# Changing the planned order of TensorE in a two-layer hybrid trunk: margins, the first tile, and where mixer outputs are reloaded

## What is computed

```python
for layer in range(2):
    xn = rmsnorm(h, mix_norm_g[layer])
    if layer == 0:
        a, xb, gate_b, gate_c = split(xn @ ab_w_in)
        mix = concat(pool_mixer(a), gate_b * short_conv(gate_c * xb)) @ ab_w_out
    else:
        u, v, q, k, w = split(xn @ cd_w_in)          # u, v through gelu
        mix = concat(u * (W_s @ layernorm(v) + b), stick_breaking_attention(q, k, w)) @ cd_w_out
    h = h + mix
    h = h + square(relu(rmsnorm(h, mlp_norm_g[layer]) @ w1)) @ w2
return rmsnorm(h, final_norm_g)
```

## Time and profile before

| | us |
|---|---|
| median of three runs | 3223.5 (3199.45 to 3227.07) |
| the profiled execution | 3217.09 |
| its span on the slowest core | 3215.6 |
| spans of the eight cores | 3180.2 to 3215.6 |
| TensorE busy in the span | 2901.0 |
| VectorE, ScalarE, POOL busy | 1450.8, 1369.0, 1136.3 |

### The profile page before, as it was taken

The page is one execution under the profiler, slowest core; times in us unless marked ns, Lnnn a source line. Parts: engine busy times, 40 slices in busy tenths (PEclk is TensorE's granted clock), DMA queues, the critical chain, the costliest instruction groups (busy, mean ns, idle before and its releaser), DMA issues.

```text
span 3215.6 us, 46006 instructions; the slowest of 8 cores (3180.2 to 3215.6 us)
## 1 busy us (share of the span) xinstructions
PE 2901.0 (90%) x14778; PEld 1258.2 (39%) x15073; DVE 1450.8 (45%) x1829; ACT 1369.0 (43%) x2273; POOL 1136.3 (35%) x1622
## 2 busy tenths in 40 slices
PE   5999788899998889889898989998999989998997
PEld 2444333344343334333343433443444433443443
DVE  4410247432445444785545363435455565554102
ACT  2435233535335445347362336242463546263442
POOL 4211016233223344654442453332254444451110
PEclk9999899999999999999999999999999999999999
DMA  7799973444657999955655243455455585555222
GB/s 161 158 173 181 171 182 71 95 102 95 164 138 125 168 184 173 187 132 129 132 120 155 83 119 85 99 111 160 110 109 109 109 198 107 110 116 177 72 76 82
DMA packets 452826, 420.46 MB, mean 131 GB/s; under 512 B 310128, under 2 KB 326768, under 8 KB 452592
## 3 DMA queue, kind: packets, MB, share of 16 engines
q1 hardware_dynamic: 383328, 228.48, 32.0%
q0 software_dynamic: 69264, 189.02, 28.1%
HBM read 304.36 MB, written 89.13 MB: 122 GB/s over the span
## 4 chain that ended last, share of the span: by engine, by line
PE 56%; DMA 18%; DVE 10%; POOL 5%; issue 5%; ACT 3%; SPq 1%; DVEq 0%; POOLq 0%; ACTq 0%
PE ps L550 52%; DMA Wk<-Wq 12%; DVE P L1197 4%; POOL Wq L1211 3%; DMA oT<-stg 2%; DMA stg<-xT 2%; PE ps L1236 2%; DMA ring<-wblk 2%; ACT ps L540 2%; PE ps L1181 1%; DVE X_45 L660 1%; POOL ps_74 L903 1%; DVE stg L671 1%; SPq L543 1%; DVE st_58 L1012 1%
## 5 line engine op out<-in xcount | busy, mean ns | idle before, releaser
L550 PE MATMUL ps<-X_45,ring 128*128 128x512 bf16 x4742 | 1101.6, 383 | 26.2 <-DVE X_45 L660 8.5
L540 ACT ACTIVATE ps<-ps 128x512 f32<-128x512 f32 (+3 forms) x832 | 576.1, 697 | 595.1 <-PE ps L550 357.4
L1211 POOL TENSOR_TENSOR Wq<-P 128x1022 bf16<-128x1022 f32 (+2 forms) x320 | 528.0, 1650 | 534.4 <-DVE P L1197 527.3
L550 PEld LDWEIGHTS ps<-X_45,ring 128*128 128x128 bf16 x4864 | 460.6, 98 | 574.9 <-issue 62.8
L1197 DVE TENSOR_TENSOR_SCAN P<-ps,carry,zeros 128x512 f32<-128x512 f32 x384 | 489.8, 1279 | 375.3 <-ACT ps L540 357.6
L550 PE MATMUL ps<-mix,ring 128*128 128x512 bf16 x2481 | 600.8, 384 | 11.0 <-issue 4.0
L581 POOL DMA_DIRECT2D ring<-wbf x540 | 297.0, 552 | 815.8 <-PE ps L550 627.4
L691 DVE TENSOR_TENSOR h<-ps,h 128x512 f32<-128x512 f32 x384 | 263.1, 686 | 703.7 <-PE ps L550 702.3
L550 PE MATMUL ps<-ffB,ring 128*128 128x512 bf16 x2009 | 482.1, 380 | 2.2 <-issue 0.2
L1197 DVE TENSOR_TENSOR_SCAN P<-ps,zeros 128x128 f32<-128x128 f32 (+3 forms) x256 | 209.0, 820 | 416.3 <-ACT ps L540 403.1
L550 PE MATMUL ps<-X_44,ring 128*128 128x512 bf16 x1498 | 358.5, 389 | 15.0 <-DVE mix L874 4.9
(11 more groups left out here) (104 smaller groups left out, 1364.9 us busy)
## 6 DMA issues: line engine op xcount, KB each, us to landing
ring<-wbf POOLq DMA_DIRECT2D x540, 256.0 KB, 4.0
ring<-wblk POOLq DMA_DIRECT2D x180, 256.0 KB, 7.4
wbf<-ring SPq DMA_DIRECT2D x180, 256.0 KB, 5.7
stg<-xT SPq DMA_DIRECT2D x96, 256.0 KB, 5.8
h<-xT SPq DMA_DIRECT2D x64, 256.0 KB, 7.7
hsp<-h SPq DMA_DIRECT2D x64, 256.0 KB, 4.6
h<-hsp SPq DMA_DIRECT2D x64, 256.0 KB, 5.1
oT<-stg SPq DMA_DIRECT2D x64, 256.0 KB, 5.3
```

The costliest lines, as they stand in the source:

```text
L540: return Req("act", lambda e: e.activation(out=out, in_=in_, func=func, **kw), reads, writes, dur, bias=bias)
L550: ins = pe.matmul(out, lhsT=l, rhs=r, start=(first and i == 0), stop=(last and i == n - 1), skip_group_check=True)
L1211: yield Req("pool", lambda e: e.tensor_tensor(out=W3[:, :, 0:w - 1], in0=P[:, :, 1:w], in1=P[:, :, 0:w - 1], op=ALU.subtract), [LP], [LWq] ...
```

## The change

It changes what the planner assumes and what some fibers ask for:

- SEM is 0.18 instead of 0.10. A new field slack adds to it for single operations: 4.0 for the AV matmul, 0.5 for the scores, 1.0 for pooling, 0.6 for the gate matmul, 3.0 for the matmul that makes the gate's bias. The transposes are planned with 5.0 us instead of 4.0.
- Norms, pooling and gate matmuls ask with a tuple, which puts them at the head of the queue for a bank; pooling and gate matmuls also get a bias of -1.0.
- prefetch_x holds its norm until the planner's TensorE is 8 us past the last square.
- At the start, x comes ahead of the gate's constants (sgst), which lie where V will be; 48 matmuls on constants come first on TensorE, and one Ln on ScalarE; the first group of the first tile takes x tile by tile; the main fiber starts when the first half of x is asked for.
- An S stage that follows an M stage reads its mixer outputs from mix, loaded while that M stage computes V, K and Q. So free_x looks for the next F stage already there, and the norm of x for the second sequence moves from the stage S(0,0) into the one of F(0,1).

```diff
-SEM = 0.10
+SEM = 0.18
@@ ready
+        far = SEM + r.slack
-                f = d.fin + (0.0 if d.eng == eng and not d.dma else SEM)
+                f = d.fin + (0.0 if d.eng == eng and not d.dma else far)
@@ Machine.advance
+            elif isinstance(y, tuple):
+                f.state = "acq"
+                y = y[0]
+                y.queue.insert(0, f)
@@ alloc
+        self.sgst, _ = sb("sgst", [128, 1536], F32, self.off)
         self.V = sb("V", [128, 16, 512], BF16)
-        self.sgst, o = sb("sgst", [128, 1536], F32, o0)
@@ norm
-        bk = yield self.banks
+        bk = yield (self.banks,)
@@ prefetch_x
-                yield self.act(X[:, c, ts], self.stg[:, b, :], AF.Square, [self.Lstg[b]], [LX[c][t]], TT, False)
+                o = yield self.act(X[:, c, ts], self.stg[:, b, :], AF.Square, [self.Lstg[b]], [LX[c][t]], TT, False)
                 self.p_stg.free(b)
+            yield lambda: self.S.free["pe"] > o.fin + 8.0
@@ start_x
+        for c in range(8):
+            yield self.load_h(self.xT, None, 0, 0, 0, c)
+        self.xloading = True
+        for c in range(8):
+            yield self.load_h(self.xT, None, 0, 0, 1, c)
...
+            if t == 1:
+                yield lambda: self.main_t >= 16
@@ free_x
-        if self.hnext is not None:
-            kind, s, u = self.hnext
-            self.M.spawn(self.prefetch_x(s, u) if kind == "F" else self.load_mix(s, u), 0.6)
+        for (k0, _, _), (kind, s, u) in zip(self.stages[n:], self.stages[n + 1:]):
+            if kind == "F":
+                self.M.spawn(self.prefetch_x(s, u), 0.6)
+                return
+            if kind == "S" and k0 == "S":
+                self.M.spawn(self.load_mix(s, u, self.X[0], self.LX[0]), 0.6)
+                return
@@ chain_pool
-            b2 = yield self.banks
-            yield self.mm(self.bank(b2), [(self.cb[:, 384 + g * 128:512 + g * 128], PB[:])], [self.Lcb, L1], [self.Lbank[b2]])
+            b2 = yield (self.banks,)
+            yield self.mm(self.bank(b2), [(self.cb[:, 384 + g * 128:512 + g * 128], PB[:])], [self.Lcb, L1], [self.Lbank[b2]],
+                          bias=-1.0, slack=1.0)
@@ stage_F
+                    fine = (s, u, i, b, t) == (0, 0, 0, 0, 0)
@@ chain_v
-            b2 = yield self.banks
+            b2 = yield (self.banks,)
...
-            yield Req("pe", fn, [Lvn, self.Lwmt], [self.Lbank[b2]], 0.25)
+            yield Req("pe", fn, [Lvn, self.Lwmt], [self.Lbank[b2]], 0.25, bias=-1.0, slack=0.6)
@@ stage_M
+        if self.stages[sn + 1][0] == "S":
+            self.M.spawn(self.load_mix(*self.stages[sn + 1][1:], self.mix, self.Lmix, lambda: self.cdone == 2), -0.2)
         yield from self.need_attention(2 * s + u)
@@ att_item
-                  bias=-1.0)
+                  bias=-1.0, slack=0.5)
...
-                  key=("wk", k), lat=4.0, kb=w * 0.69)
+                  key=("wk", k), lat=5.0, kb=w * 0.69)
...
-        yield Req("pe", fn, [LWk] + [self.LV[c * 4 + j] for j in range(nb)], [self.Lbank[self.AVB]], nb * 0.115, bias=-1.0)
+        yield Req("pe", fn, [LWk] + [self.LV[c * 4 + j] for j in range(nb)], [self.Lbank[self.AVB]], nb * 0.115, bias=-1.0,
+                  slack=4.0)
@@ stage_S
-        yield from self.out_proj("S", s, u)
-        self.free_x()
+        src = (self.mix, self.Lmix) if self.stages[n - 1][0] == "M" else (self.X[0], self.LX[0])
+        yield from self.out_proj("S", s, u, *src)
+        if src[0] is self.X[0]:
+            self.free_x(n)
@@ setup
-        self.use_scratch("init")
+        bk = yield self.banks
+        yield Req("act", lambda e: e.activation(out=self.rtmp[:, 0, 0:1], in_=self.cf[:, 72:73], func=AF.Ln), [self.Lcf],
+                  [self.Lrt[0]], 1.5)
+        yield self.mm(self.bank(bk), [(self.cb[:, 0:128], self.cb[:, 384:896])] * 48, [self.Lcb], [self.Lbank[bk]])
+        self.banks.free(bk)
+        yield lambda: self.xloading
         yield self.dma(self.sgst[:], self.sg_d, [], [self.Lsgst], "sg", kb=768.0)
```

More of the change, by code:

```diff
@@ L543, in dma, with mm @@
         return Req("sp", lambda e: e.dma_start(out=out, in_=in_), reads, writes, 0.06, key=key, lat=2.0, kb=kb)
-    def mm(self, out, pairs, reads, writes, first=True, last=True, bias=0.0):
+    def mm(self, out, pairs, reads, writes, first=True, last=True, bias=0.0, slack=0.0):
         def fn(pe):
@@ L552, in fn @@
             return ins
-        return Req("pe", fn, reads, writes, len(pairs) * 0.2157, bias=bias)
+        return Req("pe", fn, reads, writes, len(pairs) * 0.2157, bias=bias, slack=slack)
     def block_order(self):
@@ L682, in norm_h @@
         yield lambda: ev[0] == 8
-        yield from self.norm(self.X[1], self.LX[1], t, None, gcol, dst)
+        yield from self.norm(self.X[1], self.LX[1], t, gcol, dst)
         done.add(t)
@@ L721, in dst @@
                 self.p_stg.free(b)
-            yield from self.norm(X, LX, t, None, 0, dst)
+            yield from self.norm(X, LX, t, 0, dst)
             self.xready.add((s, u, t))
@@ L727, in start_x @@
         X, LX = self.X[0], self.LX[0]
-        for t in range(2):
-            ts = slice(t * TT, (t + 1) * TT)
-            for c in range(8):
-                yield self.load_h(self.xT, None, 0, 0, t, c)
+        for c in range(8):
[3 more added lines that the diff above has]
+            yield self.load_h(self.xT, None, 0, 0, 1, c)
         for t in range(2):
@@ L736, in start_x @@
                 yield self.act(X[:, c, ts], self.h[:, c, ts], AF.Square, [self.Lh[c][t]], [LX[c][t]], TT, False)
-            yield from self.norm(X, LX, t, None, 0, self.to_X(t, 0))
+            if t == 1:
+                yield lambda: self.main_t >= 16
+            yield from self.norm(X, LX, t, 0, self.to_X(t, 0))
             self.xready.add((0, 0, t))
@@ L945, in stage_F @@
                 evs = (self.chain_pool(g, t, pp, seq0, tn),) + self.chain_conv(i, t, {"cv": cv}, seq0, tn)
+                L = [LX[k][t] for k in range(8)]
                 for b in range(4):
-                    yield from self.group(self.wpairs(sl[b], X, ts), [self.Lring[sl[b]]] + [LX[k][t] for k in range(8)],
-                                          evs[b])
+                    fine = (s, u, i, b, t) == (0, 0, 0, 0, 0)
+                    yield from self.group(self.wpairs(sl[b], X, ts), [self.Lring[sl[b]]] + ([] if fine else L), evs[b],
+                                          fine=L if fine else None)
                     if t == 1:
                         self.release(sl[b])
-        self.free_x()
-        yield from self.out_proj("F", s, u)
+        self.free_x(n)
+        yield from self.out_proj("F", s, u, self.mix, self.Lmix)
         nd = set()
@@ L988, in out_proj @@
             ts = slice(t * TT, (t + 1) * TT)
-            if kind == "F":
-                src, Lsrc = self.mix, self.Lmix
-                yield lambda: self.mixn[t] == 8 and self.hcount.get((kind, s, u, t)) == 8
-            else:
-                src, Lsrc = self.X[0], self.LX[0]
-                yield lambda: (s, u, t) in self.mready and self.hcount.get((kind, s, u, t)) == 8
+            yield lambda: (self.mixn[t] == 8 if kind == "F" else (s, u, t) in self.mready) and \
+                self.hcount.get((kind, s, u, t)) == 8
             for c in range(8):
@@ L1303, in setup @@
         bk = yield self.banks
-        yield self.mm(self.bank(bk), [(self.cb[:, 0:128], self.wmt[:])], [self.Lcb, self.Lwmt], [self.Lbank[bk]])
+        yield self.mm(self.bank(bk), [(self.cb[:, 0:128], self.wmt[:])], [self.Lcb, self.Lwmt], [self.Lbank[bk]],
+                      slack=3.0)
         for g in range(4):
@@ L1321, in main @@
             if kind == "F":
-                yield from self.stage_F(s, u)
+                yield from self.stage_F(n, s, u)
             elif kind == "M":
-                yield from self.stage_M(s, u)
+                yield from self.stage_M(n, s, u)
             else:
-                yield from self.stage_S(s, u)
+                yield from self.stage_S(n, s, u)
     def build(self):
```

31 lines of the change are left out of this document (17 added, 14 removed).

## The result

The changed kernel takes 3095.4 us (median of four runs, 3089.0 to 3098.3) where the kernel before, run beside it, takes 3217.0: a ratio of 0.9625, 95% interval 0.9575 to 0.9674, 122 us saved. Predicted were 3085 us in 3035 to 3165.

What follows compares the result with a forecast made beforehand. TensorE and its 314.6 us of waits bound the kernel. From 3217.1 us, -96 - 14 - 30 - 5 + 10 - 4 + 3 = -136 gives 3081, put at 3085 us for the median; range 3035 to 3165.

Steps and rivals of the forecast that it cites:

- AV, -96: Attention's last matmul waits 123.0 us for transposed weights Wk; going later in the order gains 96 us (60 to 115).
- the clock, -30: TensorE's granted clock: 110 us less idling at 0.28 us each gains 30 us (0 to 42).
- It is no fixed price: TensorE's lower clock loses 87 us over 314.6 idle us, 0.28 each; two stages show 0.38 and 0.
- Moved loads, +3 (0 to 20): Loads of x leave S(0,0) for a quieter stage, where they stand ahead of transposes: 3 us lost (0 to 20).
- the wait moves on: TensorE meets the next late producer (normed tiles, squares, conv, pooling); half of 96 us returns: 3142 us, chance 0.22.
- Gates, +10: Gate matmuls take a bank early; 21 of 32 stand one group earlier; 8 halves lose 10 us (0 to 38).
- banks run short: 104 small matmuls hold PSUM banks before their data is there, costing 240 us: 3311 us, chance 0.06.
- The sign of being wrong: On TensorE: the forecast is wrong if waits for evacuations of PSUM banks appear; no size given.
- Next norm, -14: Next unit's norm matmul, held until 8 us past the last square, no longer waits: 14 us gained (5 to 15.6).
- start, -5: Kernel start: x ahead of sgst, first group tile by tile, against warm-up and late sgst: 5 us gained (-10 to +7).
- The row that the prediction set against the rule: At 878 to 885 us a group fed tile by tile is followed by a clock of 0.53.
- Pooling, -4: Pooling matmuls, where waits for pb_76 and pb_73 cost 15.8 us: 4 us gained (0 to 15).

Runs made afterwards that it cites:

- AV's margin alone: Kernel before, with only slack 4.0 for the AV matmul and transposes planned with 5.0 instead of 4.0 us: ratio 0.9741, 3128 us.
- both parts: Kernel before, with AV's slack 4.0, transposes planned at 5.0 us, mixer outputs reloaded in the M stage and the earlier norm of x: ratio 0.9614, 3087 us.
- the old start: Changed kernel with the start of the kernel before: sgst ahead of x, no warm-up matmuls, no early Ln, first group not tile by tile: ratio 0.9635.
- All but the reload: Changed kernel with the moved loads put back: mixer outputs loaded inside the S stages, second sequence's norm of x in S(0,0): ratio 0.9811, 3157 us.
- all but AV's margin: Changed kernel with the AV matmul's slack back at 0 and transposes planned with 4.0 us: ratio 0.9872, 3173 us.
- SEM back: Changed kernel with SEM at 0.10 instead of 0.18, all slacks kept: ratio 0.9688, 3117 us.

## Why the prediction was right, and where it was right by luck

The time was right; the sum behind it had two terms wrong by about 40 us each, in opposite directions. That they cancelled was luck.

**AV, -96, and most of the clock, -30.** Waits for Wk fell by 113 us in the change and by 100 alone (in the mean of the cores by 102 and 92), within the bounds (60 to 115). But 96 us of idling and its 0.28 of clock, 123 us together, is too much for this part: alone it gave 83. The step that failed is the price of the clock. Idle time per core fell by 75 us with AV's margin alone, from 260 to 185 in the mean of the cores by the rows of waits, and the mean granted clock not at all. 19.4 us of quicker work came in the end, but with the reload. The table shows a part of the reason: with AV's margin alone F(1,0) keeps a long wait, and the lower clock takes 17 us there; with both parts it takes 7. That is 10 of the 28 us by which the two kernels differ in clock; for the other 18 no cause was shown. "It is no fixed price" was written, and a price then used. Part of the 87 us was moreover never lost: a stretch at 0.50 in which TensorE is idle anyway (1292 to 1306 us above) counts fully in (1 - clock) x span and costs no work. In the kernel before 20 of the 87 us fall on such idle time.

**Moved loads, +3 (0 to 20).** Wrong in sign, by the most. This part is worth 11 us alone and 41 beside AV's margin. The prediction looked at what the moved transfers cost where they arrive, and priced the relief of the stage that they leave at nothing, although its DMA share of 0.94 and its transposes of 6.4 us stood in the earlier trace rows. Where they arrive they cost the transposes nothing that shows: beside 32 such loads the 48 of F(0,1) land in a median of 3.7 us, before in 3.6. It also left out the deadline of the transfers: before, x for F(1,0) had the time of AV's waits. Take those away and x comes 7.4 to 10.1 us late. Among the late producers of its rival "the wait moves on", the scaled x is not named.

**Rival "the wait moves on", 3142 us.** AV's margin alone comes near that time (3128 us), and the mechanism is there: squares 53.4 to 66.0 us, normed tiles up, a new wait for scaled x. But it is smaller than the rival had it: of 92 us that AV waits less (mean of the cores) 17 come back, not half, and the rest of the shortfall is the clock. The reload takes away the wait for scaled x alone; squares (59.8 us) and normed tiles (37.0) are waited for with both parts too.

**Gates, +10.** Right in size, wrong in reason. The waits rose by 9.7 us and the part costs 13; the four M stages are 11 us longer than with both parts alone. It is the bias, not the bank taken ahead. Nor does it act in eight half stages, as the term had it: by the main matmuls ahead of each, 15 of the 32 gate matmuls stand earlier than before, not the 21 that the section on the change counts, and 12 of these are the first halves of three stages. The rival "banks run short" falls with the order, in which the bank taken ahead moves at most 4 operations. The sign of being wrong that goes with it showed, but small: what main groups and norms wait for evacuations (into mix, by VectorE and ScalarE, of the gates' banks, vt at L1044, and into h) went from 11.9 to 24.5 us, in the mean of the cores from 10 to 18 (13 with both parts alone), where that rival had 240. The Trainium skill's rule that independent matmul groups should rotate through different PSUM banks ("Perfetto Trace Analysis", section "Matmuls") has at most these 8 us as its weight here.

**Next norm, -14; start, -5.** The wait of 10.89 us is gone. F(0,0) is 371 us against 380 with both parts alone, 3 of the 9 from the start: -6 and -3.

**Warm-up.** The Trainium skill's rule ("TensorE: Matmul & The Clock Gate", section "What's actually happening") that activity releases the clock would, as the prediction worked it out, have given 4.3 us on two norms and a group. The trace agrees for the first norm (7 matmuls in 1.89 us, 8 in 3.57 with the old start). The group fed tile by tile takes 4.56 us for 7, and the second norm is back at 3.57 for 8. The row that the prediction set against the rule decided it.

**Pooling, -4.** In all the wait fell by 6.9 us (4.1 of the 15.8 were one wait of a main group at the start), but it is opposite by its own part: pooled tiles are waited for 1.6 us with AV's margin and the reload alone, 8.9 with the whole change, and F(0,1) and F(1,1) are 9 us longer. That the bias does this, as at the gates, was not tried alone. S(1,1) is 3 us longer (268, 265 with both parts). On TensorE's timeline of the changed kernel its output projection waits for a bank that the adds into h (L696) empty, because VectorE stands ahead of these adds at L676, for a stg buffer:

```profile
2813.43 3.15 PE L555 MATMUL ps<-X_44,ring 128*128 128x512 bf16 x7 [5.60 <-DVE h L696]
```

VectorE's timeline just before it:

```profile
2809.67 0.75 DVE L676 SCALAR_TENSOR_TENSOR stg<-h,cfs,ms 128x512 f32<-128x512 f32 x1 [4.29 <-DMA oT<-stg]
```

**What stays open.** All but the reload is slower than AV's margin alone (0.9811 and 0.9741). The table puts 11 us of it at the gates, 19 at F(1,0) and 9 at the other F stages, against gains of 16 in F(0,0) and 4 in S(0,0). Which row of the change makes x later still there, 19 us of wait instead of 9, was not found; it is not the held norm.

## What to carry to other kernels

In this kernel a margin ahead of a late producer paid in full only once the time that it freed was not some other transfer's slack. So before taking a stall away, list what arrives during it and by when it is needed. Parts of a change that meet in one stage have no prices of their own; 83 and 11 us were 124 together, and only the kernel with both showed it. A bias that pulls a small matmul forward and a margin that holds it back work on the same place in the order: measure the wait ahead of it (here 24 us with the bias, 1.3 without).

## What was not expected of the hardware

The same 52 transposes land in a median of 6.4 us beside 30 loads of 256 KB on the queue that also issues them, in 4.9 us without these loads. That is S(0,0), with a DMA share of 0.99 and 0.89. In F(0,1) of the changed kernel, at 0.51, 32 such loads leave the median at 3.7 us, so the same queue alone does not explain it.

And TensorE's granted clock did not follow the sum of idle time. With AV's margin alone 75 us less idling left it at 0.973, with both parts 20 us less again (165) brought 0.982; all but the reload idles less than all but AV's margin (202 and 214 us per core) at the lower clock (0.973 and 0.977). The kernels without the reload but with AV's margin, which keep a single long wait at F(1,0), stand at 0.973 and 0.974. But with SEM back there is no such wait, the waits are 166 us as with both parts, and the clock is 0.976: which waits cost clock is open.
